# One state tile per head pair: half-height products in place of a zero-padded one in an mLSTM and attention layer

## The reference, cut to what matters

```
S   = (q k^T) * D
num = inter * (q C) + S v
den = inter * (q n) + S.sum()
h   = num / max(|den|, exp(-m_t))
C_new = decay * C + sum_s w_s k_s v_s^T
n_new = decay * n + sum_s w_s k_s
```

## Time and profile before

| | us |
|---|---|
| median of 3 runs | 2578.2 (2578.08 to 2580.16) |
| the profiled execution's own time | 2578.2 |
| its span in the profile | 2575.2 |
| TensorE matmul busy | 2446.2 |
| VectorE busy | 1323.8 |
| ScalarE busy | 877.6 |

### The profile page before, as it was taken

How to read it: one execution, slowest core, us unless ns; L and a number is a source line. 1 busy time by engine, 2 the same in 40 slices (tenths; PEclk the granted TensorE clock), 3 DMA queues, 4 the chain that set the end, 5 groups by cost and what they waited for, 6 DMA issues and landing times.

```text
span 2575.2 us, 32694 instructions
## 1 busy us (share of the span) xinstructions
PE 2446.2 (95%) x13235; PEld 2066.0 (80%) x13235; DVE 1323.8 (51%) x2593; ACT 877.6 (34%) x1540; POOL 60.3 (2%) x101
## 2 busy tenths in 40 slices
PE   6998999999998999999999899999999989999997
PEld 5886788888896788888998678888778869888885
DVE  4467544446367544446265744444635675444444
ACT  3354323233334422223334333223324434222221
POOL 2000000000000000000000300000000000000000
PEclk9999999999998999999999999999999999999999
DMA  5311223233411232323411232323533112222221
GB/s 184 84 50 47 85 90 98 91 114 124 124 52 50 74 95 94 98 90 123 148 54 33 56 99 90 98 90 108 163 57 91 48 46 86 79 74 76 81 79 65
DMA packets 176402, 224.74 MB, mean 87 GB/s; under 512 B 16299, under 2 KB 127060, under 8 KB 176236
## 3 DMA queue, kind: packets, MB, share of 16 engines
q1 hardware_dynamic: 164700, 190.34, 24.1%
q10 hardware_dynamic: 6560, 22.55, 2.5%
q0 software_dynamic: 4992, 9.76, 1.6%
HBM read 211.30 MB, written 12.60 MB: 87 GB/s over the span
## 4 chain that ended last, share of the span: by engine, by line
PE 85%; DVE 8%; ACT 3%; issue 2%; DMA 2%; ACTq 0%; SPq 0%; DVEq 0%
PE ps L1806 26%; PE ps L1808 25%; PE ps L1807 25%; PE ps L1883 2%; DVE w_lo L1018 2%; DMA w_raw<-in_w_in_dram 2%; PE ps L1863 1%; PE ps L1872 1%; ACT w_hi L608 1%; PE ps L1901 1%; DVE x L1022 1%; PE ps L1844 1%; DVE a_lo L1022 1%; ACT PT L648 1%; PE ps L1927 0%
## 5 line engine op out<-in xcount | busy, mean ns | idle before, releaser
L1806 PE MATMUL ps<-a_hi,w_hi 128*128 128x512 f32 (+2 forms) x1688 | 594.2, 352 | 29.0 <-DVE a_lo L1022 14.1
L1808 PE MATMUL ps<-a_hi,w_lo 128*128 128x512 f32 (+2 forms) x1688 | 594.2, 352 | 0.0
L1807 PE MATMUL ps<-a_lo,w_hi 128*128 128x512 f32 (+2 forms) x1688 | 593.2, 351 | 0.0
L608 ACT ACTIVATE w_hi<-w_raw 128x1024 fp32r<-128x1024 f32 (+2 forms) x368 | 365.9, 1035 | 637.3 <-PE ps L1808 575.9
L1018 DVE TENSOR_TENSOR w_lo<-w_raw,w_hi 128x1024 fp32r<-128x1024 f32 (+2 forms) x368 | 438.1, 1200 | 201.4 <-ACT w_hi L608 200.7
L1806 PE MATMUL ps<-w_hi,u_hi 128*128 128x512 f32 (+1 forms) x1088 | 431.1, 396 | 10.4 <-DVE x L1022 10.4
L1808 PE MATMUL ps<-w_hi,u_lo 128*128 128x512 f32 (+1 forms) x1088 | 430.7, 396 | 0.0
L1807 PE MATMUL ps<-w_lo,u_hi 128*128 128x512 f32 (+1 forms) x1088 | 429.9, 395 | 0.0
L1806 PEld LDWEIGHTS ps<-a_hi,w_hi 128*128 128x128 f32 x1688 | 322.4, 191 | 74.6 <-issue 21.4
L1807 PEld LDWEIGHTS ps<-a_lo,w_hi 128*128 128x128 f32 x1688 | 320.5, 190 | 41.9
L1808 PEld LDWEIGHTS ps<-a_hi,w_lo 128*128 128x128 f32 x1688 | 320.4, 190 | 40.3
(11 more groups left out here) (309 smaller groups left out, 1932.5 us busy)
## 6 DMA issues: line engine op xcount, KB each, us to landing
w_raw<-in_w_up_dram SPq DMA_DIRECT2D x128, 512.0 KB, 3.6
w_raw<-in_w_down_dram SPq DMA_DIRECT2D x128, 512.0 KB, 3.5
w_raw<-in_w_out_dram SPq DMA_DIRECT2D x32, 512.0 KB, 4.0
w_raw<-in_w_in_dram SPq DMA_DIRECT2D x24, 580.0 KB, 3.9
w_raw<-in_w_in_dram SPq DMA_DIRECT2D x24, 512.0 KB, 4.0
w_raw<-in_w_in_dram SPq DMA_DIRECT2D x32, 256.0 KB, 3.2
x<-in_x_prompt_dram ACTq DMA_DIRECT2D x12, 512.0 KB, 6.7
wide<-in_x_prompt_dram ACTq DMA_DIRECT2D x12, 512.0 KB, 4.1
```

The costliest lines, as they stand in the source:

```text
L608: eng.activation(w_hi[b][:, k * n:(k + 1) * n], raw[p % RAW][:, 0:n], ACT.Copy).then_inc(w_high.sem, 1)
L1806: eng.matmul(out, lh, rh, start=(k == ks[0]), stop=False)
L1807: eng.matmul(out, lh, rl, start=False, stop=False)
L1808: ins = eng.matmul(out, ll, rh, start=False, stop=(k == last))
```

## The change

`Cst` loses the index for the head in the pair: it holds head 2i in partitions 0 to 63 and head 2i + 1 in partitions 64 to 127 of the same 129 columns, without zeros. In `numerators` each head has two products of its own over the same output columns: first `ST` by `vm` (128 rows), then `qI` by `Cst` over the head's 64 rows. So a block's order on TensorE goes from [pair product, `ST`, `ST`] twice to [`ST` 128 rows, `qI` 64 rows] four times. The bank is chosen by the head's half (`ps[2 + par]`), where it was by the pair, and `heads` reads with a stride of 2 for that. `update_state` takes two instructions over 128 partitions where it had four over 64. The outputs of the state are read from the new layout. `srow`, a work area for the sample rows, gets memory of its own; it shared that of `Mrel`.

```diff
-        Cst = sb("Cst", [P, 2, 2, DV + 1])
+        Cst = sb("Cst", [P, 2, DV + 1])
...
+        srow = sb("srow", [HM, 5, NS])
...
-        srow = Mrel[:, :, :].rearrange("p j t -> p (j t)")[:, 0:5 * NS].rearrange("p (i t) -> p i t", i=5)
...
-                    rowsp = Cst[par * DK:(par + 1) * DK, :, par, :]
+                    rowsp = Cst[par * DK:(par + 1) * DK, :, :]
...
                 for b in range(2):
-                    ins = tt(st[:, 112 + 2 * b:114 + 2 * b], num[b][:, :, DV], cols[:, 0, j, 2 * b:2 * b + 2], ALU.max)
+                    ins = tt(st[:, 112 + b:116:2], num[b][:, :, DV], cols[:, 0, j, b:HM:2], ALU.max)
...
                 for b in range(2):
-                    ins = eng.scalar_tensor_tensor(st[:, 112 + 2 * b:114 + 2 * b], num[b][:, :, DV], -1.0, st[:, 112 + 2 * b:114 + 2 * b], ALU.mult, ALU.max)
+                    ins = eng.scalar_tensor_tensor(st[:, 112 + b:116:2], num[b][:, :, DV], -1.0, st[:, 112 + b:116:2], ALU.mult, ALU.max)
...
                 for b in range(2):
-                    ins = tt(om4[:, 2 * b:2 * b + 2, :], num[b][:, :, 0:DV], og[:, 2 * b:2 * b + 2, :], ALU.mult)
+                    ins = tt(om4[:, b:HM:2, :], num[b][:, :, 0:DV], og[:, b:HM:2, :], ALU.mult)
...
-                    for par in range(2):
-                        rs = slice(par * DK, (par + 1) * DK)
-                        ins = eng.scalar_tensor_tensor(Cst[rs, i, par, :], Cst[rs, i, par, :], st[rs, at:at + 1], ps[6][rs, i * (DV + 1):(i + 1) * (DV + 1)], ALU.mult, ALU.add)
+                    ins = eng.scalar_tensor_tensor(Cst[:, i, :], Cst[:, i, :], st[:, at:at + 1], ps[6][:, i * (DV + 1):(i + 1) * (DV + 1)], ALU.mult, ALU.add)
...
-                for i in range(2):
-                    both_heads = ps[2 + i][:, 0:2 * (DV + 1)]
-                    eng.matmul(both_heads, qI[:, i, :], Cst[:, i, :, :].rearrange("p g e -> p (g e)"), start=True, stop=False)
-                    for par in range(2):
-                        out = ps[2 + i][:, par * (DV + 1):(par + 1) * (DV + 1)]
-                        ins = eng.matmul(out, ST[:, 2 * i + par, :], vm[:, j, 2 * i + par, :], start=False, stop=(par == 1))
+                for h in range(HM):
+                    i, par = h // 2, h % 2
+                    rs = slice(par * DK, (par + 1) * DK)
+                    out = ps[2 + par][:, i * (DV + 1):(i + 1) * (DV + 1)]
+                    eng.matmul(out, ST[:, h, :], vm[:, j, h, :], start=True, stop=False)
+                    ins = eng.matmul(out, qI[rs, i, :], Cst[rs, i, :], start=False, stop=True)
                 ins.then_inc(n_out.sem, 1)
```

## The result

The changed kernel takes 2601.6 us (median of 4 runs, 2598.74 to 2605.16) against 2578.1 us: ratio 1.0092, 95% interval 1.0079 to 1.0104. Slower, as forecast, but by 23.4 us where 9.3 were forecast, and outside the range of 2582 to 2594. The profiled execution took 2601.34 us, with a span of 2599.2 us.

What follows compares the result with a forecast made beforehand. TensorE was taken to bound the kernel, except where it waits for VectorE in blocks 0 and 3. Quarters of 2.1, 2.1, 1.6 and 3.6 us made 9.3 us with two decimals carried: 2578.2 + 9.3 = 2587.5 us, range 2582 to 2594.

Steps and rivals of the forecast that it cites:

- What bounds the kernel: State stage: TensorE's time counts in blocks 1 and 2, VectorE's in block 3; block 0 has TensorE waits of 0.91 and 0.61 us.
- Columns and passes: In `numerators`: 16 passes of 129 columns at 0.11 us, 1.76 us against 1.78 before, so nothing saved.
- A change of rows, 0.20 us: Inside `numerators`: each switch between 128 and 64 rows costs 0.20 us, seven a block, 1.40 us.
- `update_state`, 0.71 us less a block: On VectorE: two instructions of 0.36 us each replace four taking 1.42 us, so 0.71 us less.
- Block 3's thin cover, 0.1 us: In block 3, `numerators` would end at 218.79 where `heads` starts at 218.73, making it 0.1 us late.
- The last quarter's eighth change: Last quarter's block 3: VectorE waits for the sample rows' projection step behind `numerators`, so all 1.60 us is exposed.
- The sum: Over the four quarters: 2.1, 2.1, 1.6 and 3.6 us more, 9.3 us with two decimals carried, giving 2587.5 us.
- The step that failed: Rival: TensorE's clock halves because `numerators` stands still, 13 us more; chance 0.12 together with dearer changes.
- dearer changes: Rival in `numerators`: changes of rows cost 0.30 us each, about 21 us, 2599; chance 0.12 together with the slow clock.
- The rival's own figure (13 us more): Slow-clock rival: a fall lasting eight 512-column products costs 1.6 us in each of eight exposed blocks; chance 0.12 with dearer changes.
- The clock pays it back: Rival behind block 3: TensorE's idle 6.57 us shrinks to 4.4, shorter half-clock stretches return 2.4 to 4.9 us; chance 0.15.

Runs made afterwards that it cites:

- grouped: The changed kernel with all four `ST` products first, then all four `qI` products, one change of rows in `numerators`: 2569.5 us, ratio 0.9968 to the kernel before.
- pairs: The changed kernel with two `ST` products, two `qI` products, and the same again, three changes of rows: 2572.4 us, ratio 0.9983 to the kernel before.
- dense: grouped with seven more 136-column products of `ST` by `vm` between its two groups, outputs unread: 2589.9 us, ratio 1.0046 to the kernel before.
- grouped_four: grouped with `update_state` in four instructions over 64 partitions again: 2577.5 us, ratio 1.0011 to the kernel before.
- changed_again: The changed kernel, unaltered, profiled once more in a single execution: 2599.1 us.
- gaps_eight: The kernel before with four products of 4 rows by 2 columns put into each block's `numerators`, eight changes of rows: 2620.7 us, ratio 1.0173.

## Why the prediction was wrong

- **What bounds the kernel:** right. Blocks 1 and 2 are TensorE's, block 0 has a wait to lose, behind block 3 VectorE's chain goes on.
- **Columns and passes:** right, 0.11 us a pass of 129 columns whatever the rows, as long as they run one after another.
- **A change of rows, 0.20 us:** right, shown by 0.42 for two passes and by the step from grouped to pairs.
- **`update_state`, 0.71 us less a block:** too small; 0.94, since I took the four instructions' mean and not what the new ones occupy, which was not to be had before.
- **Block 3's thin cover, 0.1 us:** right, 0.08. **The last quarter's eighth change:** right, the wait for the sample rows is there.
- **The sum:** 9.3 us forecast, 7.8 in the stage of dense, the kernel with the same length and no falls. So the terms that were in the sum are about right; the measured 23.4 needs one that it carried at nothing.
- **The step that failed:** "Or the granted clock goes to 0.50 (1.2 GHz) because `numerators` stands still", put aside with "Against it: TensorE stood still for about 1.5 us from 192.9 to 194.9, and the passes behind kept their length", and given a chance of 0.12 together with dearer changes. That stretch is a single stop between two dense ones, and it doesn't bear on many small stops. The new `numerators` stands still in small pieces for the same sum in each of four blocks, with `relate`'s changes right behind. The clock was at half for 30.7 us of the stage, and that costs 13.4 us against dense, 11.6 by the medians. The rival's own figure (13 us more) was about right, in part by luck: it put one fall into each of the eight blocks 1 and 2, where the profile has seven of 3.4 us and one of 6.8, three of the eight in block 0. Its chance was too small. grouped_four shows, in one execution, that even a stop in block 0 of the kind that I took as proof against can bring a fall.
- **The clock pays it back:** not shown. TensorE's idle time behind block 3 went to 4.47 us (forecast 4.4), and the slow time after the restart from 19.5 us to 13.0 in the profiled execution. But it was 17.9 us in changed_again with 4.46 us of idle time, and 19.6 in dense with 4.49. Either way it is small beside the falls in the stage. The slow stretches of dense behind the restarts, the first quarter and the sum (windows as above):

```profile
229.80:235.50 5.70, 5.70 (x14) 4.44 (x15) 3.20 (x10) 0.84 (x2) 0.00 (x0) 0.50 0.23 78
...
sum 19.60, PE 19.59 PEld 15.40 DVE 11.38 ACT 3.36 POOL 0.00; mean PE 4.90 PEld 3.85 DVE 2.85 ACT 0.84 POOL 0.00
```

- **Still open:** how falls depend on the pattern of stops; only the counts 0, 1, 3, 5, 6, 7 and 8 of changes were tried, most with one profile each. Whether it is the standing still at a change or the change itself: dense has fewer of both, and no run has many changes with little standing still; the fall behind a plain wait in grouped_four speaks for the standing still. Whether 64-row products add to it: gaps_eight shows that they aren't needed, not that they do nothing.

## What to carry to other kernels

Sort products by the number of rows of their operands before counting columns: alternating 128 and 64 rows cost 0.20 us at each switch, grouped they cost one switch and the 64-row halves ran side by side. When a change puts many small stops into TensorE's work, give the granted clock a term of its own in the sum, even where the profile will call TensorE busy throughout: here it was 13.4 of 21.1 us. And look for a reordering before dropping an edit that came out slower: with the order alone changed, the same layout is 0.32% faster than the kernel before.

## What was not expected of the hardware

The clock fell with TensorE busy for 45.80 of 45.80 us by the profile, since the first pass behind a change is drawn longer (`qI`'s passes have 0.37 and 0.27 us in turn), so busy time doesn't show these stops. The Trainium skill says that the clock is set by how busy TensorE has been of late (TensorE: Matmul & The Clock Gate, What's actually happening); the runs don't contradict it, but the profile's busy time isn't the measure: it was the whole stretch in the changed kernel (45.80 of 45.80 us, clock 0.93) and in dense (42.60 of 42.60 us, clock 1.00) alike. Two VectorE updates of 128x129 occupy 0.51 us, 0.25 each, where the four of 64x129 with alternating halves of the partitions occupied 0.36 each; the durations (0.34 us) are the same. Of the four, each started about 0.015 us after the one before had ended; of the two, the second started 0.09 before the end of the first. So here again the starts told what the durations didn't.
